# Weighted one-hots of the first key on GpSimd, between its gathers, in place of three ScalarE steps

## The reference, cut to what matters

```python
expert = e1 * N_KEYS + e2                       # e1, e2 in 0..127: the two keys of a slot
gate = jax.nn.softmax(sc, axis=-1)
act = jax.nn.gelu(jnp.einsum('td,thkd->thk', xb, u_tab[expert]), approximate=False)
return jnp.einsum('thk,thkd->td', gate * act, v_tab[expert])
```

## Time and profile before

| | |
|---|---|
| median of 3 runs | 4586.28 us (4582.92 to 4589.30) |
| the profiled execution, its own time | 4582.22 us |
| its span, first to last instruction | 4580.5 us |
| busy, share of the span | PE 72%, PE weight load 57%, DVE 64%, ACT 33%, POOL 40% |
| part 0 | 1475 to 1759 us |
| parts 1, 2, 3 | 1759, 2009, 2263 to 2518 us |
| parts 4, 5, 6 | 2518, 2824, 3123 to 3422 us |
| parts 7 to 11 and the tail | 3422 to 4581 us |

### The profile page before, as it was taken

One profiled execution on the slowest core, in us unless ns is written; L12 is line 12 of the kernel. 1 busy time (PEld: TensorE's weight loads), 2 busy tenths in 40 slices (PEclk: granted clock), 3 DMA queues, 4 the chain that ended last, 5 costly groups with the idle time before them and its releaser, 6 DMA issues.

```text
span 4580.5 us, 45717 instructions
## 1 busy us (share of the span) xinstructions
PE 3318.6 (72%) x15470; PEld 2600.0 (57%) x15470; DVE 2918.2 (64%) x6176; ACT 1526.9 (33%) x3710; POOL 1822.0 (40%) x1471
## 2 busy tenths in 40 slices
PE   4888889987756213435343899999999799989834
PEld 4877778876454213424242677777777566555511
DVE  2455554454152998888788776776768865565576
ACT  2122222222111004767586655566660001000022
POOL 1000000000001666666666554555555555454474
PEclk9999999999767655556555999999999899999967
DMA  5000000000014778888888999999999998898785
GB/s 149 6 15 15 15 15 1 15 15 10 13 35 137 253 234 272 298 311 289 307 302 298 370 347 362 346 363 366 357 351 357 378 363 312 310 397 300 290 303 217
DMA packets 394145, 1041.26 MB, mean 227 GB/s; under 512 B 57367, under 2 KB 162359, under 8 KB 390826
## 3 DMA queue, kind: packets, MB, share of 16 engines
q0 software_dynamic: 202752, 738.29, 44.1%
q1 hardware_dynamic: 179652, 249.53, 15.9%
q10 hardware_dynamic: 11510, 50.44, 2.8%
HBM read 977.06 MB, written 62.03 MB: 227 GB/s over the span
## 4 chain that ended last, share of the span: by engine, by line
PE 30%; DMA 17%; DVE 10%; POOL 6%; issue 2%; SPq 1%; ACT 1%; DVEq 1%; ACTq 0%; POOLq 0%
PE pbank L1569 23%; DMA expert_rows<-in_peer_u_dram,expert_all 8%; DMA v_blocks<-in_peer_v_dram 8%; POOL expert_rows L1492 6%; DVE expert_rows L1935 3%; PE pbank L1530 3%; PE pbank L1556 2%; PE pbank L1598 2%; DMA c_two<-h_after_mixer 1%; DVE wq_sb L1943 1%; DVE top_idx L1847 0%; DVE top_idx L1854 0%; SPq L1449 0%; DVE onehot L1888 0%; DVE onehot L1884 0%
## 5 line engine op out<-in xcount | busy, mean ns | idle before, releaser
L1492 POOL DMA_INDIRECT expert_rows<-in_peer_u_dram,expert_all x1088 | 1425.9, 1311 | 1004.0 <-DVE dots L1935 687.2
L1935 DVE CUSTOM_DVE_ANT_0 expert_rows<-expert_rows,c_two 128x1024 f32<-128x1024 f32 x1088 | 1295.8, 1224 | 397.3 <-DMA expert_rows<-in_peer_u_dram,expert_all 383.9
L1569 PE MATMUL pbank<-v_blocks,w_chunks 128*128 128x512 f32 x3072 | 1379.4, 606 | 104.2 <-DMA v_blocks<-in_peer_v_dram 101.2
L1569 PEld LDWEIGHTS pbank<-v_blocks,w_chunks 128*128 128x128 f32 x3072 | 940.3, 310 | 483.6 <-issue 148.6
L1556 PE MATMUL pbank<-slot_onehots 128*128 128x128 f32 x1536 | 285.5, 347 | 328.9 <-ACT slot_onehots L1717 274.9
L1492 POOL DMA_INDIRECT expert_rows<-in_peer_v_dram,expert_all x320 | 373.0, 1166 | 308.1 <-DVE wq_sb L1943 134.3
L347 POOL MEMSET w_in_sb<- 128x4096 f32 x1 | 3.5, 3511 | 1233.4 <-PE mbank L406 1233.4
L1556 PEld LDWEIGHTS pbank<-slot_onehots 128*128 128x128 f32 x1536 | 260.1, 252 | 376.4 <-issue 312.1
L1711 ACT ACTIVATE slot_onehots<-iota,slot_rows 128x128 f32<-128x128 f32 x1536 | 467.7, 390 | 7.3 <-ACT weight_stage L1726 7.3
L1530 PE MATMUL pbank<-cT_sb,wq_sb 128*128 128x128 f32 x2304 | 303.3, 299 | 14.9 <-ACT weight_stage L1726 7.9
L1530 PEld LDWEIGHTS pbank<-cT_sb,wq_sb 128*128 128x128 f32 x2304 | 300.4, 216 | 22.2 <-ACT cT_sb L1675 10.2
(11 more groups left out here) (367 smaller groups left out, 4221.6 us busy)
## 6 DMA issues: line engine op xcount, KB each, us to landing
v_blocks<-in_peer_v_dram SPq DMA_DIRECT2D x256, 512.0 KB, 7.6
spread_weights<-weight_stage ACTq DMA_DIRECT2D x24, 2048.0 KB, 10.2
w_chunks<-spread_weights SPq DMA_DIRECT2D x64, 768.0 KB, 18.4
expert_rows<-in_peer_u_dram,expert_all POOLq DMA_INDIRECT x1088, 6.8
wq_sb<-in_peer_wq_dram SPq DMA_DIRECT2D x4, 2048.0 KB, 18.1
w_in_sb<-in_w_in_dram SPq DMA_DIRECT2D x8, 768.0 KB, 12.2
expert_rows<-in_peer_v_dram,expert_all POOLq DMA_INDIRECT x320, 8.1
c_two<-h_after_mixer SPq DMA_DIRECT2D x9, 512.0 KB, 6.1
```

The source lines that it names most:

```text
L1492: g.indirect_dma_start(rows[:, n % RING, :], None, u_tab if kind == "u" else v_tab, bass.IndirectOffsetOnAxis(ap=idx[:, at:at + 1], axis=0 ...
L1569: m = t.matmul(bank[2 * i + b][:, :], wc[:, k % 2, i * P:(i + 1) * P, r], vb[:, n % 4, b * 512:(b + 1) * 512], start=(e == 0), stop=(e == ...
L1935: v.tensor_tensor_reduce(out=rows[:, n % RING, :], in0=rows[:, n % RING, :], in1=c[:, i % 2, :], scale=1.0, scalar=0.0, op0=ALU.mult, op1= ...
```

## The change

GpSimd makes the weighted one-hots of the first key. One `tensor_scalar` for each token compares the iota with the token's first keys and multiplies by the slots' weights, both operands being one number per partition. The instruction for token k - 8 stands behind the gather of slot k, and those of the last 8 tokens behind the gather of slot 127. Before token 0 GpSimd waits for `slots_T`, and before each fourth token for the TensorE piece that used this half of `ab` two pieces ago. TensorE waits for both halves. ScalarE keeps the half of the second key: four |iota - key| and one relu over 512 columns. The first keys and weights are copied as they are, the second keys negated.

```diff
+            def weighted(i, tok):
+                n, q = divmod(tok, 4)
+                if tok == 0:
+                    pool.wait_ge(s["sm_sb"], jobs["eT", i] + 1)
+                if q == 0 and n >= 2:
+                    pool.wait_ge(s["sm_ps"], jobs["G", i, n - 2] + 1)
+                m = g.tensor_scalar(ab[:, n % 2, 0, q, :], iota[:, :], eT[:, 1, tok:tok + 1], eT[:, 0, tok:tok + 1],
+                                    ALU.is_equal, ALU.mult)
+                if q == 3:
+                    m.then_inc(s["a_ready"], 1)
...
                     g.indirect_dma_start(rows[:, n % RING, :], None, u_tab if kind == "u" else v_tab,
                                          bass.IndirectOffsetOnAxis(ap=idx[:, at:at + 1], axis=0)).then_inc(got[n % RING], 16)
+                    if build_tile(p) is not None and k >= 8:
+                        weighted(build_tile(p), k - 8)
+                if build_tile(p) is not None:
+                    for k in range(SLOTS - 8, SLOTS):
+                        weighted(build_tile(p), k)
...
                 pe.wait_ge(s["ab_ready"], i * 32 + n + 1)
+                pe.wait_ge(s["a_ready"], i * 32 + n + 1)
...
-                ac.activation(eT[:, 0, :], src[:, 0:P], ACT.Copy)
-                ac.activation(eT[:, 1:3, :], src[:, P:3 * P].rearrange("p (f t) -> p f t", f=2), ACT.Copy, scale=-1.0).then_inc(s["sm_sb"], 1)
+                if i > 0:
+                    act.wait_ge(s["a_ready"], i * 32)
+                ac.activation(eT[:, 0:2, :], src[:, 0:2 * P].rearrange("p (f t) -> p f t", f=2), ACT.Copy)
+                ac.activation(eT[:, 2, :], src[:, 2 * P:3 * P], ACT.Copy, scale=-1.0).then_inc(s["sm_sb"], 1)
...
-                both = ab[:, n % 2, :, :, :]
-                for f in range(2):
-                    for q in range(4):
-                        ac.activation(both[:, f, q, :], iota[:, :], ACT.Abs, bias=eT[:, 1 + f, 4 * n + q:4 * n + q + 1])
+                b = ab[:, n % 2, 1, :, :]
+                for q in range(4):
+                    ac.activation(b[:, q, :], iota[:, :], ACT.Abs, bias=eT[:, 2, 4 * n + q:4 * n + q + 1])
                 act.drain()
-                flat = both.rearrange("p f q e -> p (f q e)")
-                ac.activation(flat, flat, ACT.Relu, scale=-1.0, bias=one[:, :])
-                act.drain()
-                for q in range(4):
-                    m = ac.activation(both[:, 0, q, :], both[:, 0, q, :], ACT.Copy, scale=eT[:, 0, 4 * n + q:4 * n + q + 1])
-                m.then_inc(s["ab_ready"], 1)
+                ac.activation(b, b, ACT.Relu, scale=-1.0, bias=one[:, :]).then_inc(s["ab_ready"], 1)
```

More of the change, by code:

```diff
@@ L1364, in peer_block @@
         names = ("p_consts k_in keysT_ps keysT_sb rms c_ready idx_ready dots_done gate_exp gelu_done w_ready "
-                 "sm_ps sm_sb ab_ready spilled vb_used vacc_free h6_in hs_in late_in p_in acc_done "
+                 "sm_ps sm_sb a_ready ab_ready spilled vb_used vacc_free h6_in hs_in late_in p_in acc_done "
                  "gate_rms en_ready sum_ready rms2 y_ready y_out h8_zero").split()
```

## The result

| | before | with the change |
|---|---|---|
| median, four runs each | 4584.60 us (4568.72 to 4589.30) | 5070.91 us (5048.19 to 5074.98) |
| ratio, 95% interval | | 1.1057 (1.1015 to 1.1100) |
| span of the profiled execution | 4580.5 us | 5071.8 us |
| parts 1, 2, 3 | 250, 254, 255 us | 351, 357, 352 us |
| parts 4, 5, 6 | 306, 299, 299 us | 365, 362, 370 us |

The forecast was 4770 us in a range of 4640 to 5050. The direction, the place and the kind of the loss came as forecast; the size did not, and the measured time lies 21 us above the range, near rival B (5037 us). By the profiles parts 1 to 3 lost 300 us together and parts 4 to 6 lost 193; the rest of the kernel changed by under 5 us.

A forecast was written before the change was run, and what follows sets the result against it. Buffer, gather, row and dot loop bounds parts 1 to 3, TensorE part 6; GpSimd was to become the bound at 2.31 us a slot. 4582.22 + 159 (parts 1 to 3) + 29 (parts 4 to 6) = 4770 us, range 4640 to 5050.

The forecast's parts named there:

- rival B: GpSimd's one-hot is dear, 0.83 + 0.1 us of its own: 2.68 us a slot, 5037 us in all; chance 0.20.
- ScalarE's relief: ScalarE loses about 116 of a part's 181 us; nothing in the chain waits for this, so it counts 0.
- waits for a running dot: A GpSimd gather or one-hot reading SBUF waits for VectorE's dot to end: 0.27 us each, ends 0 and 1.05.
- A gather was put at 1.25 + 0.27 = 1.52 us a slot: On GpSimd, 1.25 us from gather to gather with no dot running, plus 0.27 us of waiting for dots.
- GpSimd becomes the bound of parts 1 to 3: At 2.31 us a slot GpSimd takes 296 us for 128 slots, over the 250 to 255 of today.
- the one-hot's own 0.42 + 0.1 us: Each one-hot on GpSimd costs 0.42 us, taken from the 128x128 select, plus 0.1 for a gap: 0.52 us.
- 0.27 us of waiting for dots: Gathers' mean wait of 0.32 us, scaled for thinner dots to 0.27, for each gather and each one-hot on GpSimd.
- The waits on top, 10 us a part: GpSimd loses 4 us a part waiting for `eT` and 6 us to VectorE's bursts of choosing experts.
- 5 us a part for the tie: Parts 4 to 6: TensorE (299 us) and GpSimd (306) wait for each other and rows come later, so 311 each.
- C: One-hots do not meet dots, only gathers do: 2.04 us a slot, 271 us a part, 4651 us; chance 0.18.
- D: Not slower: one-hots run in the 53.9 us GpSimd waits for VectorE, so the time stays at 4582; chance 0.07.
- E: A gain: ScalarE's copies reach TensorE sooner in parts 4 to 6, 3 us a part, 4573 at most; chance 0.03.

The follow-up runs named there:

- the 2 x 2 of one-input dots: Each dot replaced by a sum over the row alone, in the kernel before and in the changed kernel: 4515.8 and 4655.2 us.

## Why the prediction was wrong

**Right.** That ScalarE's relief is worth little held in the run with the relief alone, a ratio of 0.9978 with an interval that holds 1; that it is worth nothing is not shown. That a GpSimd instruction which reads SBUF waits for a running dot was read from two gathers, and the 2 x 2 of one-input dots shows it. A gather was put at 1.25 + 0.27 = 1.52 us a slot and came at 1.51, in other shares: 1.02 + 0.17 undisturbed, 0.28 for dots and 0.04 for VectorE's releases. That GpSimd becomes the bound of parts 1 to 3, and its waits for VectorE nearly vanish, came so too.

**The term that failed first: the one-hot's own 0.42 + 0.1 us.** It measured 0.80 + 0.04, which is 0.32 us of the missing 0.48 a slot. I had two rows for it, named the missing row for two operators, and still took the select's 0.42. The swap to multiply and add, whose price is what I had assumed, puts parts 1 to 3 at 927 us together, against the forecast's 918; with the real pair they take 1059. So in these parts most of the miss goes with that number. That the swap lands so near is in part luck: its instruction waits 0.54 us and not 0.27, its gathers cost 1.39 and not 1.52 with their gaps, and the 10 us of waits on top did not come. Rival B had the own cost at 0.83 + 0.1, and with it 353 us a part and 5037 us. Parts 1 to 3 did take 353, but with less own cost (0.84), more waiting (0.44 for its 0.25) and without its 10 us on top, so B's nearness is in part luck too.

**The term that failed second: 0.27 us of waiting for dots, "for gather and one-hot alike".** The gather waits 0.28, but the one-hot 0.44, the other 0.17 us a slot. A gather is held up by no more than one dot's length (2.08 us), a one-hot by up to three (4.0 us). With constants in place of the per-partition operands the excess falls to 0.24 and the longest to 1.74, so the long waits go with the operands. That is where my step was blind, since the trace of before holds no instruction of this kind. I had put the ends of the wait at 0 and a gather's 1.05 us. For the mean this held (0.44, and 0.74 with half of the one-hots on GpSimd); single one-hots waited up to 3.2 us.

**The waits on top, 10 us a part, did not come in parts 1 to 3.** GpSimd waits 5 to 7 us a part for VectorE, which its 1.51 us a slot contain, and 0.6 us at most for `eT`. The sum of slots alone is the part. In part 6 alone it waits 10.3 us for `eT`.

**Parts 4 to 6: 5 us a part for the tie.** They came at 366 against 353 in parts 1 to 3, so 13; the waits for TensorE are under 4 us a part of that, and a third buffer takes nothing measurable off. TensorE needed 299 before and GpSimd needs 353, so that "the slower plus a little" was the right form here, on a wrong base. Had my base been right, the form would have failed: in the run with multiply and add GpSimd needs 309 us by parts 1 to 3, and parts 4 to 6 take 341. That is 32 us a part and not 5: some 9 of waiting for TensorE, 3 for `eT`, and 18 for row buffers that VectorE releases late. The tie was priced alone, and of "rows come later" my sum had no term.

**The other rivals.** C (one-hots do not meet dots) is refuted by the change's own one-hots of up to 4.0 us, beside 0.83 us on the mean with one-input dots. The one-input run took 271 us a part and 4655 us, where C had 271 and 4651, but that is luck: C had gathers that wait and one-hots of 0.52 us, the run gathers that do not wait and one-hots of 0.84. D (one-hots in GpSimd's spare) is answered by the run with half of them: the spare is real and is filled, but already half of the one-hots make the part 44 us longer. E is bounded at half a percent. ScalarE was to lose 116 us a part and lost 90. Most of this miss is that its 128x128 instructions overlap: 1536 of 390 ns keep it busy for 467.7 us, 0.30 each; and a relu over 512 columns takes 722 ns, not half of 1149. Nothing hangs on it. Nor on the 0.2 us by which I had dots held up in turn, which were 0.03 on the mean in parts 1 to 3.

The range broke at its upper end, 5050, because it was built to hold B only just, while the own cost and the waiting were both in doubt and both to the same side: B's own cost with the measured 0.44 of waiting gives 1.51 + 0.93 + 0.44 = 2.88 us a slot, an estimate beyond B's 2.68.

## What to carry to other kernels

An engine's spare is to be taken from the stretch and not from the page: GpSimd was at 40% of the span and at 79% of the parts in question, gaps between gathers included. Before work is moved to GpSimd, ask what VectorE runs beside it: instructions with two SBUF inputs held up every kind of GpSimd instruction here that reads SBUF, and the one with per-partition operands for up to three of them in a row. And an instruction that the trace does not have is to be timed by itself for its own pair of operators; the nearest shape had half the cost here.

## What the runs showed of the hardware

- On GpSimd, over 128x128 float32, start to start: multiply and add with two per-partition operands 0.43 us, compare and multiply 0.77, multiply alone 0.58, is_equal alone 0.58, copy 0.25. Fewer operators are not always cheaper.
- A memset on GpSimd beside back-to-back dots keeps its 0.22 us; a compare with constants goes from 0.67 to at most 1.74, one with per-partition operands from 0.80 to at most 4.0, an indirect DMA from 0.94 to at most 2.08 in the change and 2.20 in any run. The Trainium skill's "SBUF — State Buffer", section "Who interferes with whom", says that only GpSimd instructions that read are met by a VectorE instruction with two inputs; the memset, and the dots with one input, agree. In its section "Summary: rules for kernel authors" the page lets the second one to issue wait until the first finishes; the one-hot of 2338.66, which ends after three dots, shows more than that.
- Dots are held up in turn, but little: 1246 ns for 1224 on the mean, and 1.57 us at most.
- The gap ahead of a gather is 0.30 us after another gather and 0.17 us after a one-hot, and an undisturbed gather takes 0.94 and 1.02 us.
